# Hybrid decoder step on one core: norms of queries and keys by two reciprocals, the first branch gate of later tiles between the gathers, tile 0 weighed in four strips

## The reference, cut to what matters

```python
h = _rmsnorm(x, g_pre_mix) * (1.0 + sc1) + sh1
proj = h @ w_in          # aq, ak, av, conv_in, a_dec, b_beta, z, g_a, g_b
o_att = sliding-window attention(q, k, v, sinks, rel_bias)
dq, dk_, dv_ = split(silu(short_conv(conv_in)))
q = _l2norm(dq) * DK ** -0.5;  k = _l2norm(dk_)     # x * rsqrt(sum(x * x) + eps), per head
o_d = gated delta rule(q, k, dv_, g_log, beta, s0), in chunks
o_d = _rmsnorm(o_d, delta_norm) * silu(z)
merged = sigmoid(g_a) * (o_att @ w_att_out) + sigmoid(g_b) * (o_d @ w_delta_out)
x = x + gt1 * _rmsnorm(merged @ w_out, g_post_mix)
h2 = _rmsnorm(x, g_pre_ffn) * (1.0 + sc2) + sh2
f: per token and head, the 16 best of 128 x 128 experts by h2 @ w_query and sub_keys;
   sum over experts of gate * gelu(h2 . expert_u[e]) * expert_v[e]
x = x + gt2 * _rmsnorm(f, g_post_ffn)
```

## Time and profile before

| | us |
|---|---|
| median of 3 runs | 1861.95 |
| lowest and highest run | 1859.13, 1863.99 |
| span of the profiled execution | 1860.3 |

### The profile page before, as it was taken

One profiled execution on the slowest core, in us unless ns is written; L12 is line 12 of the kernel. 1 busy time (PEld: TensorE's weight loads), 2 busy tenths in 40 slices (PEclk: granted clock), 3 DMA queues, 4 the chain that ended last, 5 costly groups with the idle time before them and its releaser, 6 DMA issues.

```text
span 1860.3 us, 22142 instructions
## 1 busy us (share of the span) xinstructions
PE 1459.1 (78%) x7786; PEld 684.7 (37%) x7786; DVE 1249.6 (67%) x2827; ACT 688.9 (37%) x1775; POOL 612.5 (33%) x590
## 2 busy tenths in 40 slices
PE   8999999999898896788877566666666676666666
PEld 4777878988544463333322101101111110000002
DVE  3077657886876658766767667777667677667665
ACT  3145455312444537524323222432322243222223
POOL 1100000000343244344345444454444444444442
PEclk9999999999999897799898767867666776676766
DMA  9533343206799999999999999999999999999997
GB/s 356 171 130 109 128 138 132 74 24 238 297 421 420 413 420 422 376 420 403 424 421 415 425 423 424 423 421 425 424 418 424 422 421 414 418 421 423 417 423 312
DMA packets 99903, 643.28 MB, mean 346 GB/s; under 512 B 11730, under 2 KB 11898, under 8 KB 31781
## 3 DMA queue, kind: packets, MB, share of 16 engines
q0 software_dynamic: 76912, 555.82, 72.3%
q1 hardware_dynamic: 22688, 85.96, 12.6%
q10 hardware_dynamic: 192, 0.09, 0.0%
HBM read 636.65 MB, written 6.18 MB: 346 GB/s over the span
## 4 chain that ended last, share of the span: by engine, by line
PE 40%; DMA 39%; DVE 9%; ACT 7%; issue 4%; POOL 1%; SPq 0%; ACTq 0%; DVEq 0%; POOLq 0%
DMA arena<-in_euv,consts 38%; PE abank L900 22%; PE dbank L900 5%; PE fsum L1635 4%; DVE arena L2368 4%; PE dbank L1635 4%; ACT consts L866 2%; POOL arena L473 1%; ACT L864 1%; ACT small L864 1%; PE fsum L964 1%; ACT L769 1%; ACT arena L746 1%; PE abank L1528 1%; ACT arena L490 1%
## 5 line engine op out<-in xcount | busy, mean ns | idle before, releaser
L2368 DVE CUSTOM_DVE_ANT_0 arena<-arena 128x1024 f32<-128x1024 f32 x520 | 633.8, 1224 | 399.8 <-DMA arena<-in_euv,consts 398.9
L473 POOL DMA_INDIRECT arena<-in_euv,consts x520 | 577.7, 1111 | 765.9 <-PE fsum L1635 370.1
L900 PE MATMUL abank<-arena 128*128 128x256 f32 (+4 forms) x2392 | 526.7, 378 | 5.1 <-ACTq L748 2.8
L1635 PE MATMUL dbank<-arena,consts 128*32 128x512 f32 x1024 | 360.6, 838 | 213.3 <-ACT consts L866 212.5
L900 PEld LDWEIGHTS abank<-arena 128*128 128x128 f32 (+1 forms) x2392 | 389.3, 191 | 161.6 <-issue 70.8
L1635 PE MATMUL fsum<-arena,consts 128*32 128x512 f32 x1024 | 298.9, 778 | 162.8 <-ACT consts L866 162.0
L864 ACT ACTIVATE small<-small 128x1 f32<-128x1 f32 x520 | 104.8, 202 | 675.4 <-DVE small L2368 669.6
L1635 PEld LDWEIGHTS dbank<-arena,consts 128*32 128x32 f32 x1024 | 42.0, 123 | 494.8 <-ACT consts L866 483.6
L490 ACT ACTIVATE arena<-abank 128x512 f32<-128x512 f32 (+5 forms) x228 | 111.7, 490 | 256.8 <-PE abank L900 243.9
L866 ACT ACTIVATE consts<-arena,small 128x32 f32<-128x32 f32 x520 | 167.1, 321 | 16.9
L1635 PEld LDWEIGHTS fsum<-arena,consts 128*32 128x32 f32 x1024 | 37.8, 120 | 365.1 <-ACT consts L866 346.5
(11 more groups left out here) (335 smaller groups left out, 1193.2 us busy)
## 6 DMA issues: line engine op xcount, KB each, us to landing
arena<-in_wstream SPq DMA_DIRECT2D x132, 512.0 KB, 5.7
arena<-in_euv,consts POOLq DMA_INDIRECT x520, 13.2
arena<-in_wout SPq DMA_DIRECT2D x8, 1024.0 KB, 9.5
arena<-in_x SPq DMA_DIRECT2D x5, 512.0 KB, 6.4
arena<-in_sdel POOLq DMA_DIRECT2D x1, 2048.0 KB, 9.6
out_deltas<-arena POOLq DMA_DIRECT2D x1, 2048.0 KB, 12.3
out_yp<-arena SPq DMA_DIRECT2D x4, 512.0 KB
arena<-mod SPq DMA_DIRECT2D x3, 512.0 KB, 11.1
```

What stands on the lines that cost most here:

```text
L473: pool.indirect_dma_start(ring[n % SLOTS], None, I["euv"], bass.IndirectOffsetOnAxis(cur[:, u % 2, c:c + 1], 0)).then_inc(ring_in[n % SLOT ...
L900: return pe.matmul(out, lhsT, rhs, start=first, stop=last)
L1635: last = pe.matmul(out[e][to:to + 32, :], weighed, v, start=h == 0 and kk == 0, stop=h == PH - 1 and kk == 3, skip_group_check=True)
L2368: TTR(uh, uh, rep[j] if t < NT else h2sb, 1.0, 0.0, ALU.mult, ALU.add, dot[:, n // NQ % 2, n % NQ:n % NQ + 1]).then_inc(s.dots_done, 1)
```

## The change

- The sums of squares go into strips: head m's sum lands on partitions 32 * (m % 4) and following, by a matmul with 32 columns of ones. ScalarE takes the roots of the strips into one tensor for queries and one for keys. VectorE takes two reciprocals, one for each. TensorE then copies each head's row to all partitions, with a matmul over one row, for two parts of 8 heads (`roots_copied`), and VectorE multiplies from PSUM.
- The sums are no longer interleaved with modulation and gates. Behind them come, with `roots_copied` after the second and third step, five steps of modulation blocks and gates: (4, 1), (4, 1), (4, 2), (0, 2), (0, 8).
- The a gate is computed for tile 0 alone in the front. For later columns its 8 weight blocks are fetched again, and it is computed between the gathers, where each channel block has an a gate and a b gate at ticks 9 to 33. The attention's projection for later columns is copied to `gaT` by ScalarE, and VectorE multiplies it there with the gate.
- All b gates but the last four stand before the chunk preparation.
- Mixing starts at tick 34 in place of 26; norms, turns and queries follow, closer together. The first scores of tile 1 are split into two heads' halves.
- A weighed v of tile 0 is added by four matmuls of 256 columns into four strips in place of two of 512 into two strips; ScalarE collects the sums in 11 copies in place of 3.
- A few waits and one buffer move: SP waits for `mod_out` in place of VectorE, `mgt` lies elsewhere.

```diff
-BEHIND, AHEAD = [5, 1, 1, 1] + [1] * B_CONV, [1, 2] * DH
+BEHIND, AHEAD = [5, 1, 1, 1] + [1] * B_CONV, [(4, 1), (4, 1), (4, 2), (0, 2), (0, 8)]
...
-        mgt = at(X0, 2, 512)
+        mgt = at(R0 + D, 2, 512)
...
-        GATE_FROM, MIX_FROM = 9, 26
+        MIX_FROM = 34
...
-        GATE_AT = {GATE_FROM + 2 * m: m for m in range(KT)}
-        FIRST_AT = {GATE_FROM - 1 + 2 * m: PH + m for m in range(PH)}
-        NORMAL = {37: 0, 38: 1, 40: 2, 42: 3}
-        SECOND = {39: 0, 41: 1, 43: 2, 44: 3}
-        TURN = {41: 0, 43: 1, 45: 2, 46: 3}
-        ROWS_LATER = {48: 1, 50: 2, 52: 3}
-        QUERY = {(47 + 2 * m if m < 8 else 64 + 3 * (m - 8)): m for m in range(2 * PH)}
+        GATE_AT = {i: g for g, i in enumerate((9, 11, 13, 15, 17, 18, 20, 21, 23, 24, 26, 27, 29, 30, 32, 33))}
+        FIRST_AT = {i: PH + m for m, i in enumerate((8, 10, 12, 14, 16, 19, 22, 25))}
+        NORMAL = {45: 0, 46: 1, 47: 2, 48: 3}
+        SECOND = {47: 0, 48: 1, 49: 2, 50: 3}
+        TURN = {48: 0, 49: 1, 50: 2, 51: 3}
+        ROWS_LATER = {53: 1, 55: 2, 57: 3}
+        QUERY_AT = (52, 53, 54, 55, 57, 58, 59, 62, 64, 67, 70, 73, 76, 79, 82, 85)
+        QUERY = {i: m for m, i in enumerate(QUERY_AT)}
...
-        N_AGAIN = N_QRY + B_QRY + B_GB
+        N_AGAIN = N_QRY + B_QRY + B_GA + B_GB
...
             for m in range(2 * DH):
-                if m >= 2:
-                    act.wait_ge(s.l2_done, m - 1)
+                strip = slice(32 * (m % DH), 32 * (m % DH) + 32)
                 for lo, hi in PARTS:
                     b = sums.to_read()
-                    step(A(rnb[:, m % 2, lo:hi], b[:, 0:hi - lo], ACT.Sqrt, bias=eps128 if m < DH else eps,
+                    step(A(rnb[strip, m // DH, lo:hi], b[strip, 0:hi - lo], ACT.Sqrt, bias=(eps128 if m < DH else eps)[strip],
                            scale=float(P) if m < DH else 1.0), s.dring_free)
...
+                if 2 <= lv < 2 + B_ATT:
+                    for c in range(2):
+                        empty(gaT[:, 2 * (lv - 2) + c, P:TOK], slice(0, TOK - P))
...
             for m in range(2 * DH):
                 pe.wait_ge(s.sq_ready, m + 1)
+                strip = slice(32 * (m % DH), 32 * (m % DH) + 32)
                 for lo, hi in PARTS:
                     b = dring.to_fill()
-                    mm(b[:, 0:hi - lo], ones, sqb[:, m % 2, lo:hi]).then_inc(s.dring_full, 1)
-                modulation(AHEAD[m])
-                gate()
-                if m == 0:
+                    mm(b[strip, 0:hi - lo], ones[:, 0:32], sqb[:, m % 2, lo:hi]).then_inc(s.dring_full, 1)
+
+            def roots_copied(half):
+
+                pe.wait_ge(s.sq_ready, 2 * DH + half + 1)
+                for r in range(0, P, 32):
+                    for lo, hi in PARTS:
+                        b = dring.to_fill()
+                        mm(b[:, 0:hi - lo], ones[r:r + 1, :], rnb[r:r + 1, half, lo:hi]).then_inc(s.dring_full, 1)
+
+            for n, (ahead, blocks) in enumerate(AHEAD):
+                modulation(ahead)
+                for _ in range(blocks):
+                    gate()
+                if n == 0:
                     values_weighed(NT - 1)
+                if n in (1, 2):
+                    roots_copied(n - 1)
...
-                    pe.wait_ge(s.merged_ready, KT)
+                    pe.wait_ge(s.merged_ready, 2 * KT)
...
+                    if t == 0:
+                        for e in range(4):
+                            v = ring[n % SLOTS][:, D + 256 * e:D + 256 * e + 256]
+                            bank, strip = e // 2, (j + e) % NQ
+                            first = (bank, strip) not in strips_begun
+                            strips_begun.add((bank, strip))
+                            last = pe.matmul(out[bank][32 * strip:32 * strip + 32, 256 * (e % 2):256 * (e % 2) + 256], weighed, v,
+                                             start=first, stop=h == PH - 1 and kk == 3, skip_group_check=True)
...
-            for m in range(2 * DH + 1):
-                if m < 2 * DH:
-                    dve.wait_ge(s.silu_out, m + 1)
-                    step(TT(sqb[:, m % 2, :], ct[:, m, :], ct[:, m, :], ALU.mult), s.sq_ready)
-                if m == 1:
-                    for c in range(4, 8):
-                        modulation(c)
-                if m >= 1:
-                    dve.wait_ge(s.rn_ready, m)
-                    r = rnb[:, (m - 1) % 2, :]
-                    step(recip(r, r))
-                    step(TT(ct[:, m - 1, :], ct[:, m - 1, :], r, ALU.mult), s.l2_done)
+            for m in range(2 * DH):
+                dve.wait_ge(s.silu_out, m + 1)
+                if m >= 2:
+                    dve.wait_ge(s.dring_full, BEFORE_SUMS + 2 + 2 * (m - 1))
+                step(TT(sqb[:, m % 2, :], ct[:, m, :], ct[:, m, :], ALU.mult), s.sq_ready)
+            for half in range(2):
+                dve.wait_ge(s.rn_ready, half + 1)
+                step(recip(rnb[:, half, :], rnb[:, half, :]), s.sq_ready)
+            dring.n += 4 * DH + 2
+            step.n[s.dring_free.name] += 4 * DH + 2
+            for c in range(4, 8):
+                modulation(c)
+            for m in range(2 * DH):
+                for lo, hi in PARTS:
+                    b = dring.to_read()
+                    step(TT(ct[:, m, lo:hi], ct[:, m, lo:hi], b[:, 0:hi - lo], ALU.mult), s.dring_free)
+                dve.sem_inc(s.l2_done, 1)
```

More of the change, by code:

```diff
@@ L53, in front_order @@
         order += [block] * (m > 1) + [("ada", next(later)) for _ in range(BEHIND[m])]
-    for m, block in enumerate(GATES):
-        order += [("ada", next(later)) for _ in range(AHEAD[m - 2] if 2 <= m < 2 + len(AHEAD) else 0)] + [block]
-    return order
+    blocks = iter(GATES)
+    order += [next(blocks), next(blocks)]
+    for ahead, gates in AHEAD:
+        order += [("ada", next(later)) for _ in range(ahead)] + [next(blocks) for _ in range(gates)]
+    return order + list(blocks)
 C_ID, C_LE, C_GT, C_ONE, C_LVL, C_IOTA, C_P8, C_8P, C_E4 = 0, 128, 256, 384, 512, 1408, 1424, 1456, 1584
@@ L1197, in _ @@
             keys_and_values(0)
-            parted = weights()
-            gate_part(parted, 0)
             pe.wait_ge(s.kTs_ready, 1)
@@ L1246, in attended @@
                                 block_before_used(last)
-                        last.then_inc(s.dring_full, 1)
+                        last.then_inc(full, 1)
             def sample_state(h, g):
```

103 lines of the change are left out of this document (56 added, 47 removed).

## The result

The changed kernel took 1875.24 us in the median of four runs (1873.82 to 1880.85), the kernel before 1861.74 beside it (1859.13 to 1863.99). The ratio is 1.0081, 95% interval 1.0067 to 1.0095: 13.5 us slower, where 8 us faster was forecast. (The ratio takes in all runs; of the two medians alone it is 1.0073. So what follows from the two traces adds up to 18.7 us and not to 13.5, and where the 5 us more stand isn't known.

What follows compares the result with a forecast made beforehand. TensorE was taken to bound the kernel before the gathers, the DMA behind their start. 1860.3 - 21.3 (front) + 10.0 (bytes) + 3 (crowding) = 1852.0, put at 1853.5 us for the median; eight-in-ten range 1840 to 1867.

Steps and rivals of the forecast that it cites:

- The norm loop: TensorE's stretch from first sums to key transposes: 64.3 us where 79.9 was read, a saving of 15.6.
- two reciprocals earn nothing in themselves: VectorE before the key transposes: two reciprocals for eight save 20 us there, only keeping VectorE from being late.
- The chunk preparation: At 292 to 344 us: VectorE's two waits behind the parted a gate go, gaining 4.7 us.
- the front: Everything ahead of the first gather: 15.6 + 4.7 + 1 = 21.3 us gained, between 13 and 27.
- The bytes: Between the gathers: eight a blocks fetched a second time, 4.19 MB at 421 GB/s, cost 10.0 us uncovered.
- The crowded stretch: Ticks 45 to 60: norms, turns and queries pressed together lose 3 us of DMA time, between -4 and +12.
- crowding decides: Rival, ticks 45 to 60: ScalarE and VectorE fall behind, first search late; 12 us for 3, 1862.5; chance 0.18.
- the weak front: Rival, before the gathers: VectorE or weights hold TensorE, only some 10 of 21 us come; 1865; chance 0.10.
- The clock rival: Rival, among gates between gathers: TensorE drops to 1.2 GHz, three ticks need 32 us against 18.7; 1872; chance 0.08.
- the signs of being wrong: Weight waits over 5 us among short gates, clock under 0.9 at 520 to 650 us, or slow DMA slices.
- The sign of the DMA: Ticks 45 to 60: more than one slice of ten microseconds under 380 GB/s would show the forecast wrong.
- The strips: Tile 0's weighing between gathers: lone slots released 0.5 us sooner, under DMA; nothing gained where TensorE is behind.

Runs made afterwards that it cites:

- beta early: Changed kernel with ScalarE's chain for beta moved from behind all gates to ahead of the second z gate; ratio 1.0073.
- the bytes alone: Kernel before with eight weight blocks fetched once more at ticks 9 to 24 into an unused place, nothing computed from them; 0.64%, 11.9 us slower.
- the late plan alone: Kernel before with mixing, norms, turns and queries at the changed kernel's later ticks and tile 1's first scores in halves; ratio 1.0076.
- fewer products: Changed kernel with three of the eight products left out of each query block of the later tiles; ratio 1.0047.

## Why the prediction was wrong

**The norm loop was mis-sized by 6.2 us, and wrongly framed.** Against my 64.3 us the terms came out so. Waits for weights 5.6 us (1.68, 2.02, 1.92) for 2.5. Short gates 5.46 + 19.76 = 25.2 for 21.6, the modulation blocks 1.92 + 1.92 + 3.60 = 7.4 for 6.2. The sums took 8.5 for 9.5 (by the forecast's own terms, 8 x 1.08 + 1.28, it should have been 9.9) and the copies 4.06 + 3.48 = 7.5 for 8.3. My sum had no term for the clock here. TensorE was granted 0.50 from 248.5 to 252 us, 0.66 to 260 and 0.81 from 263 to 272, behind stops of 1.7 to 2.0 us; the kernel before had 1.00 from 200 to 300. At 1.00 the last four modulation blocks take 1.9 (not 3.60), two short gates 3.84 (not 5.46), ten 18.1 (not 19.76) and the first copies 3.5 (not 4.06), as other rows of the runs show: an estimated 5.5 us. So I had the waits 3.1 us too small and the clock's 5.5 not at all, and the sums 1.0 and the copies (3.5 each at 1.00) 1.4 too large. The larger fault is in the sentence that two reciprocals earn nothing in themselves but keep VectorE from being late. I never priced the loop with the gates moved and the norms left alone. By my own terms that is 8.0 + 6.2 + 14.3 + 21.6 + 1.9 = 52.0, and the run read 52.7. VectorE was then late by 6.5, but by the order of its program: with the eight reciprocals kept and the order changed the wait is 0.19. With its order mended, TensorE's way from the key transposes to the first gather is 189.1 us (264.49 to 453.6), against 184.4 with the new norms and beta early (279.66 to 464.1). So the new norms paid 15 to 18 us of TensorE in the loop to save some 5 behind it. With the old norms the moved gates alone bring the first gather 18.7 us forward, near the 21.3 that I had forecast for both.

**The chunk preparation was a missed step.** I counted 4.7 us gained by waits that end. ScalarE's beta chain, which I didn't look for, has one more wide gate behind it in the old order, 7.15 us of TensorE, and that covered it. With all gates ahead it stood bare, 5.2 us, in the trace; that mending it alone pays, the runs don't show (1.0073 against 1.0081). From the small product to the first level the changed kernel did gain some 2 us (293.50 to 340.74 us before, 288.90 to 334.16 after), and levels and merges gave 1.4 of it back. In sum the front brought 5.2 us and not 21.3.

**The bytes** were right: 10.0 worked out, 11.9 by the runs of the bytes alone, 10.7 in their profile to tick 40, of which 3.7 come back behind. 420 GB/s in the gate stretch and 140 fetches, as said.

**The crowded stretch was mis-sized, 3 us for 14.** 23.9 us behind the first gather less 10.0 of bytes are 13.9, and ticks 40 to 60 hold 13.9 more than before; the late plan alone costs 14. My sum was made for VectorE in ticks 45 to 51. There the 60 us at 385 GB/s lose 5 us, with ScalarE the busy one. The larger hole is TensorE's in ticks 52 to 62, and it is the product count: a query block of 2.90 and a slot's 0.64 in turn, and a search whose scores wait for that. With fewer products 7.8 of the 13.9 us are gone, with the search a tick later 7 behind tick 60; the rest isn't taken apart. I had put the queries under "less room" without a price. The rival "crowding decides" had the place, the late search and nearly the size, at 12, but it named ScalarE and VectorE as what falls behind, where the largest hole is TensorE's.

**The rivals were taken as exclusive.** Crowding (12 for 3) and the weak front (10 of 21) both came. Together they give 1853.5 + 9 + 11 = 1873.5, beside 1875.2 measured; that this is so near is in part luck, since in the profile the front brought 5.2 us and not 10, and neither came by quite the cause that its rival names. The chance of slower should have held their product, and I gave them only the clock. The clock rival itself, among the gathers, did not decide: 0.94 was granted from 500 to 684 us. Of the signs of being wrong, the waits for weights came to 5.6 us in the loop, but only 1.92 of them stand ahead of a short gate, so as worded that sign did not come. The sign of the DMA did: in ticks 45 to 60 three slices of ten microseconds are under 380 GB/s (317, 311, 364).

**The strips** earn nothing where the old list stands, as I said, and nothing measurable on the late plan either. Why two strips cost 0.6% more in the changed kernel is open; the profile has 2 us of it in the gathers.

## What to carry to other kernels

When a change has parts, price the kernel with each part left out; the part that is "free because hidden" may be the one that costs, since hiding it spends the critical engine's time (here 7.5 us of copies and 5.6 of waits on TensorE to save VectorE). When work is moved away from beside a small chain of another engine, look up what that chain was hidden under, and start it as early as its inputs allow; here that paid only when VectorE's order was mended too. Two rivals that act at different places add up: give their sum a chance of its own.

## What was not expected of the hardware

Copying one row to 128 partitions costs TensorE as much as a full product of that width: eight of 256 or 264 columns took 3.48 us, and eight products of 256 columns over 128 rows took 3.62. The Trainium skill (TensorE: Matmul & The Clock Gate, Step-by-step: what each phase is for) says of the loading of the weights that the row count does not matter; in these rows, which hold loads and products together, it doesn't either.

The fronts with short stops were granted less clock, and not the same each time: 0.85, 0.89 and 0.95 were granted at 205 to 345 us in kernels with the new norms, with busy shares of 85, 88 and 90%, where the old front, busy 99%, had 1.00. The first gather differs by up to 8 us among five kernels with one and the same front. That the clock alone does it isn't shown: 0.90 was granted both with the first gather at 474.3 and with it at 480.7.
